# Streaming the whole v table as tiles for the first token group, instead of gathering its v rows

## The chip, the cores and the metric

The kernel runs on one core of one Trainium2 chip. The metric is the device time of one execution in microseconds (us), as the median of several runs. A profile is one execution recorded by the hardware profiler. The engines are PE (TensorE, matrix products), DVE (VectorE), ACT (ScalarE), POOL (GpSimd) and SP (SyncE), and 16 DMA engines move data between the device memory and the on-chip memory.

## The reference

Two transformer layers run one after the other on 512 tokens of width 1024. The change is in the last part only, a product-key expert layer (`peer_ffn`). Each token picks, in each of 8 heads, the 16 best of 16,384 experts; a row of table `u` gives each expert's gate, and a row of table `v` its output:

```python
idx = jnp.take_along_axis(cand_i..., best_pos, axis=-1)      # 8 heads x 16 experts a token
g = jax.nn.softmax(best_s, axis=-1)
pre = jnp.einsum('td,thkd->thk', xt, u[idx])
coef = g * jax.nn.gelu(pre, approximate=False)
out = x + jnp.einsum('thk,thkd->td', coef, v[idx])
```

Both tables are 16,384 x 1024 in float32, 64 MiB each. An expert's number is i * 128 + j, with i and j the two halves' keys.

## The kernel before

**Tiling.** Tokens lie on the 128 partitions, so there are four token tiles (t = 0 to 3), worked in two groups of two. A chunk k is one head of one token tile: k = 8t + head, 32 chunks in all. A chunk holds 16 expert slots. One gather brings, for one slot, the chosen row of `u` or `v` for each of 128 tokens: 128 rows of 4 KB, 512 KB. So 512 gathers read `u` and 512 read `v`.

**Who does what.** POOL issues all gathers in one queue, in the order of a written-out list `SEQ` (L433 ff.; the issuing line is L568). DVE multiplies a gathered `u` tile with the token's vector and sums it (`dots`, L1043), ranks scores and picks experts (`prep_top`, 986 to 1033), and for some `v` slots scales and adds the gathered rows itself (`added`, L1072). The other `v` slots go over PE (`weighted`; its matmuls stand at the helper line L1514): ACT writes a 128 x 128 diagonal matrix of the slot's coefficients (`diagonals`, L933), and PE multiplies it with the gathered 128 x 1024 tile in two matmuls of 512 columns, which add up in PSUM. In the profile one float32 matmul is two records. `on_vector` says which slots go to DVE: before, none of the first group (chunks 0 to 15), and 4 of 16 in chunks 16 to 28, 8 of 16 in the last three.

**Order.** The `u` gathers of chunks 0 to 15 run early, beside the dense layers and attention, through six buffers. Behind them the list has `v` chunks 0 to 2, then one `u` chunk and up to two `v` chunks in turn, until the last `v` chunks. These 768 later gathers go round a ring of 23 buffers: gather n takes the buffer of gather n - 23 and waits until that one is used up. Ten of the buffers lie in the attention's keys (`FIRST_KEYS`) and seven in the layer's scratch (`FIRST_LAYER`), and these wait for the end of the work that uses the place. POOL issues in order, so a gather that waits holds back all behind it.

**The end of the dense work.** PE ends its last dense matmuls (the expert scores of the last tile) at about 1326 us of the profile. From there on only the expert part is left; below it is called the tail.

## Time and profile before

| what | value |
|---|---|
| median of 3 runs | 2462.14 us (2461.33 to 2468.46) |
| the profiled execution's own time | 2447.57 us |
| its span in the trace | 2445.8 us |
| PE busy, share of the span | 1989.4 us, 81% |
| DVE busy | 1262.6 us, 52% |
| POOL busy | 1153.6 us, 47% |
| moved by the software (POOL) queue | 537.87 MB |
| mean rate over the span | 279 GB/s |

A stretch of the trace is read with the view by windows (busy time of each engine, number of records, granted PE clock as a share of full speed, DMA share, GB/s) and then with the timeline of one engine, where each row is a start, a duration, and in square brackets how long the engine had been idle and what ended it.

### The profile page before, as it was taken

The numbers are of one execution on the slowest core, as the hardware profiler recorded it, in microseconds if no ns is written. First come the engines' busy times: TensorE is split into PE (matmuls) and PEld (weight loads), VectorE is DVE, ScalarE is ACT, GpSimd is POOL, SyncE is SP. The second block draws the span as 40 slices with busy tenths as digits, with TensorE's granted clock in tenths as the row PEclk, the third lists the DMA queues.
The fourth block names the chain that finished last, engine by engine and source line by source line (L and its number), as shares of the span: only waits on it lengthen the run. The fifth ranks groups of instructions, "written<-read, shape, count | busy, mean of one in ns | idle before, by whom it ended". The sixth has DMA issues, their size and how long they took to land.

```text
span 2445.8 us, 20834 instructions
## 1 busy us (share of the span) xinstructions
PE 1989.4 (81%) x6988; PEld 1199.1 (49%) x6988; DVE 1262.6 (52%) x3046; ACT 501.1 (20%) x1238; POOL 1153.6 (47%) x1070
## 2 busy tenths in 40 slices
PE   6999999877699998877888988898888775574666
PEld 6777666566566673655567433343333232231222
DVE  0111125355878865799758533344433355445645
ACT  1111024312011111233312212222221121121211
POOL 2000000000335544657462577767677777767675
PEclk9999998888798898966999988998898898777878
DMA  5321343256576787988797999999999999999998
GB/s 154 103 104 69 120 143 137 78 207 215 206 275 230 265 308 290 382 286 280 270 365 266 331 356 362 359 334 354 363 354 357 372 332 332 399 349 403 354 378 309
DMA packets 209050, 681.88 MB, mean 279 GB/s; under 512 B 20145, under 2 KB 20145, under 8 KB 208945
## 3 DMA queue, kind: packets, MB, share of 16 engines
q0 software_dynamic: 148032, 537.87, 59.6%
q1 hardware_dynamic: 57968, 135.80, 15.4%
q10 hardware_dynamic: 2944, 6.89, 0.8%
q8 instruction: 57, 0.93, 0.1%
q14 instruction: 49, 0.39, 0.0%
HBM read 677.33 MB, written 3.15 MB: 278 GB/s over the span
## 4 chain that ended last, share of the span: by engine, by line
PE 62%; issue 12%; POOL 8%; DVE 7%; DMA 5%; another core or an unknown queue 3%; ACT 3%; ACTq 0%; SPq 0%; DVEq 0%; POOLq 0%; PEldq 0%
PE ps L1514 60%; POOL sb_arena L568 8%; DVE sb_arena L1043 3%; DMA sb_arena<-in_peer_u,sb_idx 1%; DMA sb_arena<-in_peer_v,sb_idx 1%; DMA sb_wring<-in_w_out 1%; DMA sb_gains<-in_norm_g 1%; DVE sb_arena L1454 1%; DMA sb_wring<-in_w_in 0%; ACT sb_arena L933 0%; DMA sb_wring<-in_w_up_attn 0%; PE ps L1823 0%; DVE sb_arena L1460 0%; DVE sb_stat L1439 0%
## 5 line engine op out<-in xcount | busy, mean ns | idle before, releaser
L1514 PE MATMUL ps<-sb_arena 128*128 128x512 f32 (+6 forms) x2736 | 1066.2, 542 | 312.8 <-issue 223.6
L568 POOL DMA_INDIRECT sb_arena<-in_peer_u,sb_idx x512 | 621.0, 1213 | 1036.5 <-DVE sb_idx L1033 499.6
L1514 PEld LDWEIGHTS ps<-sb_arena 128*128 128x128 f32 (+3 forms) x2736 | 504.7, 201 | 847.5 <-issue 776.0
L1043 DVE CUSTOM_DVE_ANT_0 sb_arena<-sb_arena 128x1024 f32<-128x1024 f32 x512 | 613.4, 1224 | 342.2 <-DMA sb_arena<-in_peer_u,sb_idx 295.7
L568 POOL DMA_INDIRECT sb_arena<-in_peer_v,sb_idx x512 | 520.3, 1016 | 239.8 <-issue 145.2
L1514 PE MATMUL ps<-sb_arena,sb_wring 128*128 128x256 f32 (+2 forms) x2816 | 536.8, 352 | 42.6 <-issue 32.7
L1514 PEld LDWEIGHTS ps<-sb_arena,sb_wring 128*128 128x128 f32 x2816 | 469.2, 201 | 97.9 <-issue 38.4
L933 ACT ACTIVATE sb_arena<-sb_ident,sb_coef 128x128 f32<-128x128 f32 x436 | 169.3, 399 | 889.4 <-PE ps L1514 397.2
L1514 PE MATMUL ps<-sb_wring,sb_arena 128*128 128x512 f32 (+3 forms) x608 | 258.1, 582 | 31.4 <-DMA sb_wring<-in_w_out 10.7
L1072 DVE SCALAR_TENSOR_TENSOR sb_arena<-sb_arena,sb_coef 128x1024 f32<-128x1024 f32 x76 | 97.7, 1286 | 215.9 <-DMA sb_arena<-in_peer_v,sb_idx 139.4
L1514 PEld LDWEIGHTS ps<-sb_wring,sb_arena 128*128 128x128 f32 (+1 forms) x608 | 117.7, 197 | 162.1 <-issue 119.7
L1252 DVE TENSOR_REDUCE sb_stat<-ps 128x1 f32<-128x144 f32 (+3 forms) x32 | 16.2, 506 | 91.2 <-PE ps L1514 91.0
L1823 PE MATMUL ps<-sb_ident,sb_arena 128*128 128x128 f32 x160 | 34.1, 364 | 19.0 <-DVE sb_arena L1468 18.7
L803 ACT COPY sb_arena<-ps 128x512 f32<-128x512 f32 x36 | 21.1, 585 | 138.6 <-PE ps L1514 117.0
L1043 DVE DVE_READ_ACCUMULATOR2_ANT sb_coef<- 128x1 f32 x512 | 42.0, 82 | 0.0
L1514 PE MATMUL ps<-sb_negc,sb_eye 8*128 8x16 f32 (+4 forms) x128 | 41.7, 403 | 0.0
L1823 PEld LDWEIGHTS ps<-sb_ident,sb_arena 128*128 128x128 f32 x160 | 24.8, 190 | 25.7 <-DVE sb_arena L1468 23.0
L1426 DVE SCALAR_TENSOR_TENSOR sb_arena<-ps,sb_stat,sb_arena 128x512 f32<-128x512 f32 x16 | 12.0, 750 | 46.3 <-PE ps L1514 38.3
L682 ACT ACTIVATE sb_arena<-ps,sb_stat 128x144 f32<-128x144 f32 (+3 forms) x32 | 17.2, 538 | 72.3 <-DVE sb_stat L1252 72.3
L690 ACT ACTIVATE sb_arena<-ps 128x512 f32<-128x512 f32 x16 | 9.6, 597 | 100.9 <-PE ps L1514 100.9
L827 ACT COPY sb_arena<-ps 128x128 f32<-128x128 f32 (+3 forms) x64 | 24.0, 427 | 29.5 <-PE ps L1823 28.8
L970 DVE SCALAR_TENSOR_TENSOR sb_newton<-sb_stat 128x1 f32<-128x1 f32 (+2 forms) x23 | 3.6, 157 | 49.5 <-ACT sb_stat L592 49.5
(220 smaller groups left out, 1071.8 us busy)
## 6 DMA issues: line engine op xcount, KB each, us to landing
sb_wring<-in_w_in SPq DMA_DIRECT2D x52, 1024.0 KB, 7.5
sb_wring<-in_peer_w_q SPq DMA_DIRECT2D x32, 1024.0 KB, 8.2
sb_wring<-in_w_o SPq DMA_DIRECT2D x16, 1024.0 KB, 6.9
sb_wring<-in_w_out SPq DMA_DIRECT2D x8, 1024.0 KB
sb_arena<-in_peer_u,sb_idx POOLq DMA_INDIRECT x512
sb_arena<-in_peer_v,sb_idx POOLq DMA_INDIRECT x512
sb_arena<-in_x ACTq DMA_DIRECT2D x8, 512.0 KB, 7.9
sb_wring<-in_w_up_pool SPq DMA_DIRECT2D x4, 1024.0 KB
```

Of the source, the lines that this page charges most:

```text
L568: nc.gpsimd.indirect_dma_start(gathered[buf(n)][:], None, table, bass.IndirectOffsetOnAxis(ap=idx[:, t, s:s + 1], axis=0))\
L682: nc.scalar.activation(Pb[:, n % 2, 0:w], s_ps[:, 0:w], ACT.Exp, bias=stat[:, 96 + n % 4:97 + n % 4], accum_out=stat[:, 100 + n % 4:101 + ...
L803: nc.scalar.copy(dst, src).then_inc(prep_evac, 1)
L827: nc.scalar.copy(PT2[:, kind, 0:i + 1, :], psum[:, 4 + kind, 0:(i + 1) * P].rearrange("p (a b) -> p a b", b=P))\
L933: nc.scalar.activation(diag[:, n % 4, :], ident[:], ACT.Copy, scale=coef[:, t, s:s + 1])\
L1043: nc.vector.tensor_tensor_reduce(out=gathered[buf(n)][:], in0=gathered[buf(n)][:], in1=xn[:, t % TG, :], scale=1.0, scalar=0.0, op0=ALU.mu ...
L1072: nc.vector.scalar_tensor_tensor(rows_of_tile(t), gathered[buf(n)][:], coef[:, t, s:s + 1], rows_of_tile(t), ALU.mult, ALU.add).then_inc(v ...
L1252: nc.vector.tensor_reduce(stat[:, 96 + n % 4:97 + n % 4], s_ps[:, 0:w], AX, ALU.max, negate=True)\
L1426: nc.vector.scalar_tensor_tensor(cols, psum[:, wo_bank(i, n), :], stat[:, 82 + kind:83 + kind], cols, ALU.mult, ALU.add).then_inc(x2_added, 1)
L1454: link(nc.vector.tensor_tensor_scan(suffix[:, w - 1::-1] if w == T else suffix[:, 0:w][:, ::-1], suffix[:, w - 1::-1] if w == T else suffi ...
L1514: return nc.tensor.matmul(o, l, r, start=start, stop=stop)
L1823: last = nc.tensor.transpose(psum[:, 4 + kind, j * P:(j + 1) * P], Pb2[:, kind, j * P:(j + 1) * P], ident[:])
```

## The change

For the first group (tiles 0 and 1) the `v` rows are no longer gathered. The whole `v` table is read once, as 128 tiles of 128 consecutive rows (512 KB each; tile i holds the experts with first key i). For each tile and each of the two token tiles PE multiplies a 128 x 128 weight matrix `dense_w` (row j: the coefficient of expert 128 i + j for each token) with the tile: 4 matmuls of 512 columns a tile (`dense`).

The weights are built on the chip, in two halves of 64 tiles. `split` and `ranks` bring the two keys and the coefficients of all slots onto the partitions by token. Then, 32 times for each half, for eight tokens: DVE makes eight 128 x 128 one-hot matrices of key j in one instruction and eight 128 x 64 one-hot matrices of key i scaled with the coefficient (`picks`), PE multiplies them (`build`, 8 matmuls of 64 columns), and ACT copies the result from PSUM (`spread`).

The list now has `u` 16 and 17, five times 12 tiles and a `u` chunk (18 to 22), 4 tiles, the second build (`b`) with `u` 23, `v` 16 and 17 worked between its steps, five times a `u` chunk, 12 tiles and a `v` chunk, and a remainder with the last 4 tiles. The tiles are issued by POOL in the same queue and go round the same ring as the gathers. The ring has 18 buffers until the last tile, and 33 behind it. `on_vector` now gives DVE 8 of 16 slots of every `v` chunk but 16 and 17.

```diff
+HALF = NK // 2
+PICK = 8
+BUILDS = TG * P // PICK
...
+        SEQ = [("u", 16), ("u", 17)]
...
+        for m in range(18, 23):
+            SEQ += stream(12) + [("u", m)]
+        SEQ += stream(4) + [("b", 0), ("u", 23), ("v", 16), ("v", 17)]
+        for m in range(24, 29):
+            SEQ += [("u", m)] + stream(12) + [("v", m - 6)]
+        SEQ += [("v", 23), ("u", 29)] + stream(4) + [("v", k) for k in range(24, 27)]
+        SEQ += [("u", 30), ("v", 27), ("v", 28), ("u", 31), ("v", 29), ("v", 30), ("v", 31)]
...
-            return k >= EARLY_CHUNKS and j % (2 if k >= CHUNKS - SHARED else 4) == 1
+            return k not in WITH_BUILD and j % 2 == 1
...
+        first_ring = list(KEYS) + list(RING)
+        second_ring = list(OVER) + list(SCORES) + first_ring
...
+            if n < OPEN:
+                return first_ring[(n - LATE) % len(first_ring)]
+            return second_ring[(n - OPEN) % len(second_ring)]
...
+            elif b in OVER:
+                eng.wait_ge(d_used, NK)
...
+                if kind == "d":
+                    gp.dma_start(gathered[buf(n)], table[k * P:(k + 1) * P, :]).then_inc(tile_landed[buf(n)], 16)
...
+            def spread(b):
...
+                act.wait_ge(pick_used, b + 1)
+                if half and q == 0:
+                    act.wait_ge(d_used, HALF)
+                nc.scalar.copy(dense_w[:, :, t, at_:at_ + PICK],
+                               psum[:, 4 + b % 2, :].rearrange("p (s i) -> p i s", s=PICK)).then_inc(spread_done, 1)
...
+            def picks(b):
...
+                    dve.wait_ge(pick_used, b - 1)
+                nc.vector.tensor_tensor(pick_j[b % 2], rank_t[:, TG + t, at_:at_ + PICK].unsqueeze(2)
+                                        .to_broadcast([P, PICK, NK]),
+                                        iota[:].unsqueeze(1).to_broadcast([P, PICK, NK]), ALU.is_equal)
+                for n in range(PICK):
+                    last = nc.vector.tensor_scalar(pick_a[:, b % 2, n, :], iota[:, HALF * half:HALF * (half + 1)],
+                                                   rank_t[:, t, at_ + n:at_ + n + 1],
+                                                   rank_t[:, 2 * TG + t, at_ + n:at_ + n + 1], ALU.is_equal, ALU.mult)
+                last.then_inc(pick_done, 1)
...
+            def build(b):
+                pe.wait_ge(pick_done, b + 1)
...
+                    pe.wait_ge(spread_done, b - 1)
+                for n in range(PICK):
+                    last = mm(psum[:, 4 + b % 2, n * HALF:(n + 1) * HALF], pick_j[b % 2][:, n, :],
+                              pick_a[:, b % 2, n, :], True, True)
...
+            def dense(i):
+                if i % HALF == 0:
+                    pe.wait_ge(spread_done, BUILDS * (i // HALF + 1))
...
+                for t in range(TG):
+                    for e in range(2):
+                        last = mm(sums_of(t)[:, e, :], dense_w[:, i % HALF, t, :],
+                                  gathered[buf(n)][:, 512 * e:512 * e + 512], i == 0, i == NK - 1)
+                last.then_inc(d_used, 1)
```

On PE the tail was one row of matmuls behind the last dense ones (`ps` is PSUM, `sb_arena` the large buffer that holds gathered tiles and diagonals). Before:

```order
L1514 MATMUL ps<-sb_arena 128x128 x4
L1514 MATMUL ps<-sb_arena,sb_wring 128x128 x32
L1514 MATMUL ps<-sb_arena 128x128 x8
L1514 MATMUL ps<-sb_arena 128x512 x872
L60 UNCONDITIONAL_BRANCH
```

After, the same place has the transposes of `ranks`, the 256 small matmuls of the first build, and then the first 60 tiles at four matmuls each, some of them in buffers that lie in the weight ring `sb_wring`:

```order
L1635 MATMUL ps<-sb_arena 128x128 x8
L2062 MATMUL ps<-sb_ident,sb_arena 128x128 x4
L2067 MATMUL ps<-sb_ident,sb_coef 128x128 x2
L1635 MATMUL ps<-sb_arena 128x64 x256
L1635 MATMUL ps<-sb_wring,sb_arena 128x512 x16
L1635 MATMUL ps<-sb_arena 128x512 x48
L1635 MATMUL ps<-sb_wring,sb_arena 128x512 x40
L1635 MATMUL ps<-sb_arena 128x512 x48
```

So the first matmul on `v` data now stands behind the whole first build. Further on, in the second build, each group of 8 small matmuls has one gathered slot of chunk 16 or 17 (2 matmuls) behind it.

On POOL, behind the 256 early gathers of `u`, three `v` chunks came before the next `u` chunk. Before:

```order
L568 DMA sb_arena<-in_peer_u,sb_idx 128x1024 x256
L568 DMA sb_arena<-in_peer_v,sb_idx 128x1024 x48
L568 DMA sb_arena<-in_peer_u,sb_idx 128x1024 x16
L568 DMA sb_arena<-in_peer_v,sb_idx 128x1024 x32
L568 DMA sb_arena<-in_peer_u,sb_idx 128x1024 x16
```

After, two `u` chunks follow at once (L626, a gather, has `sb_idx` as a source), and then 12 plain tile loads (L623) between `u` chunks:

```order
L626 DMA sb_arena<-in_peer_u,sb_idx 128x1024 x266
L626 DMA sb_wring<-in_peer_u,sb_idx 128x1024 x8
L626 DMA sb_arena<-in_peer_u,sb_idx 128x1024 x10
L626 DMA sb_wring<-in_peer_u,sb_idx 128x1024 x4
L623 DMA sb_wring<-in_peer_v 128x1024 x4
L623 DMA sb_arena<-in_peer_v 128x1024 x8
L626 DMA sb_arena<-in_peer_u,sb_idx 128x1024 x2
L626 DMA sb_wring<-in_peer_u,sb_idx 128x1024 x8
```

What moved is that no transfer of `v` data stands before the 289th of the queue, and that from there on transfers that PE frees and transfers that DVE frees alternate in blocks.

## Rows read from the trace of the kernel before

**Rows 1.** Windows: us, busy (records) PE PEld DVE ACT POOL, PEclk, DMA, GB/s:
```profile
1326.50:2445.80 1119.30, 840.38 (x1744) 350.27 (x1744) 522.97 (x1075) 218.03 (x517) 783.79 (x752) 0.86 0.95 355
1326.50:1800.00 473.50, 406.69 (x888) 174.21 (x888) 199.27 (x541) 102.50 (x248) 326.10 (x321) 0.92 0.95 355
...
2100.00:2400.00 300.00, 172.33 (x323) 68.06 (x321) 157.99 (x238) 47.67 (x108) 216.01 (x214) 0.76 0.97 377
```

**Rows 2.** The chain that ended last, 1640 to 1730 us: start, duration, what:
```profile
1650.41 4.86 issue
1655.27 3.78 PE ps L1514 x4
...
1665.06 56.29 PE ps L1514 x124
1721.35 4.89 issue
```

**Rows 3.** Timeline of POOL, buffers freed by PE, then a free one:
```profile
1408.10 0.94 POOL L568 DMA_INDIRECT sb_arena<-in_peer_v,sb_idx  x1 [0.78 <-PE ps L1514]
1409.82 0.94 POOL L568 DMA_INDIRECT sb_arena<-in_peer_v,sb_idx  x1 [0.78 <-PE ps L1514]
...
1420.26 0.93 POOL L568 DMA_INDIRECT sb_arena<-in_peer_v,sb_idx  x1 [0.31 <-issue]
```

**Rows 4.** Timelines of DVE and POOL: rankings' ends, first late u chunk:
```profile
1319.90 0.17 DVE L1033 CAST sb_idx<-sb_arena 128x16 uint32<-128x16 f32 x1
1328.74 0.17 DVE L1033 CAST sb_idx<-sb_arena 128x16 uint32<-128x16 f32 x1
...
1364.28 0.17 DVE L1033 CAST sb_idx<-sb_arena 128x16 uint32<-128x16 f32 x1
...
1374.27 0.93 POOL L568 DMA_INDIRECT sb_arena<-in_peer_u,sb_idx  x1 [1.28 <-PE ps L1514]
...
1379.27 1.23 DVE L1043 CUSTOM_DVE_ANT_0 sb_arena<-sb_arena 128x1024 f32<-128x1024 f32 x1 [14.82 <-DMA sb_arena<-in_peer_u,sb_idx]
```

**Rows 5.** Timelines of DVE and POOL, a stretch of dots back to back:
```profile
1971.84 1.22 DVE L1043 CUSTOM_DVE_ANT_0 sb_arena<-sb_arena 128x1024 f32<-128x1024 f32 x1
...
1972.98 1.22 DVE L1043 CUSTOM_DVE_ANT_0 sb_arena<-sb_arena 128x1024 f32<-128x1024 f32 x1
...
1971.88 1.98 POOL L568 DMA_INDIRECT sb_arena<-in_peer_v,sb_idx  x1 [0.31 <-issue]
```

**Rows 6.** Small DVE work: timeline near 1293 us, then groups by line:
```profile
1293.70 0.17 DVE L1015 TENSOR_SCALAR sb_arena<-sb_arena 128x16 uint32<-128x16 uint32 x1
1293.78 0.17 DVE L1016 TENSOR_SCALAR sb_arena<-sb_arena 128x16 uint32<-128x16 uint32 x1
...
1294.19 0.76 DVE L1020 TENSOR_TENSOR sb_arena<-sb_arena,sb_iota 128x256 f32<-128x256 f32 x2
...
L1085 DVE TENSOR_TENSOR sb_arena<-sb_arena,ps 128x1024 f32<-128x1024 f32 x4 | 4.9, 1217 | 3.3 <-PEq L1956 3.3
```

**Rows 7.** Small matmuls: timeline of PE, then groups of 0 to 60 us:
```profile
1316.88 7.31 PE L1514 MATMUL ps<-sb_arena,sb_wring 128*128 128x128 f32 x64
...
L1514 PE MATMUL ps<-sb_arena,sb_wring 128*128 128x16 f32 x59 | 8.5, 296 | 0.0
```

**Rows 8.** View by windows: full PE clock, and small matmuls of attention:
```profile
1600.00:1650.00 50.00, 50.00 (x118) 22.04 (x116) 24.87 (x65) 13.31 (x31) 35.60 (x35) 1.00 0.93 339
...
1050.00:1100.00 50.00, 35.51 (x141) 27.12 (x140) 44.54 (x95) 19.21 (x42) 29.41 (x21) 0.60 0.76 260
```

**Rows 9.** Single rows: a copy from PSUM, a plain DMA issued by POOL:
```profile
1326.13 0.58 ACT L803 COPY sb_wring<-ps 128x512 f32<-128x512 f32 x1 [0.42 <-PE ps L1514]
...
7.58 0.55 POOL L535 DMA_DIRECT2D sb_gain_row<-in_final_norm_g  x1
```

**Rows 10.** Timelines at the end: last gather, last sum:
```profile
2430.30 1.01 POOL L568 DMA_INDIRECT sb_arena<-in_peer_v,sb_idx  x1 [0.31 <-issue]
...
2441.45 1.22 DVE L1085 TENSOR_TENSOR sb_arena<-sb_arena,ps 128x1024 f32<-128x1024 f32 x1 [3.34 <-PEq L1956]
```

More of the change, by code:

```diff
@@ L942, in _ @@
                         gelu(CHUNKS - 1, CHUNKS)
[L943 to L944 removed]
+                    for _ in diagonals(m):
+                        pass
+                elif kind == "u":
                     for _ in range(2):
@@ L1115, in experts, with split @@
                             k_w += 1
-                        continue
-                    added(k)
-                    if k % H == 4 and k > H:
-                        finish(finished_tiles)
-                        finished_tiles += 1
-                for t in range(finished_tiles, NT):
-                    finish(t)
+                    elif kind == "b":
+                        rows_ = dots(23)
+                        for b in range(BUILDS):
+                            picks(BUILDS + b)
+                            if b < TOPK:
+                                next(rows_)
+                    elif kind == "v" and k not in WITH_BUILD:
+                        added(k)
+                        if k in (26, 27, 28):
+                            finish(k - 26)
+                finish(NT - 1)
+            def split():
+                dve.wait_ge(u_used, LATE)
+                both = idx[:, 0:TG, :].rearrange("p a b -> p (a b)")
+                nc.vector.tensor_scalar(rank_u[:, 0, :], both, 7, None, ALU.logical_shift_right)
+                link(nc.vector.tensor_scalar(rank_u[:, 1, :], both, NK - 1, None, ALU.bitwise_and))
+                nc.vector.tensor_copy(rank[:], rank_u[:]).then_inc(rank_ready, 1)
+            def picks(b):
+                half, q = divmod(b, BUILDS)
+                t, at_ = divmod(q * PICK, P)
+                if b < 2:
+                    dve.wait_ge(rank_copied, 2)
+                else:
+                    dve.wait_ge(pick_used, b - 1)
[7 more added lines that the diff above has]
+                last.then_inc(pick_done, 1)
             stream = experts()
@@ L1950, in weighted @@
                     for e in range(2):
-                        last = mm(psum[:, 4 + 2 * (t % 2) + e, :], diag[:, m % 4, :],
-                                  gathered[buf(n)][:, 512 * e:512 * e + 512], s == 0, s == last_row)
+                        last = mm(sums_of(t)[:, e, :], diag[:, m % 4, :],
+                                  gathered[buf(n)][:, 512 * e:512 * e + 512], row == 0, row == last_row)
                     last.then_inc(v_used, 1)
-                    if s == last_row:
+                    if row == last_row:
                         pe.wait_ge(v_used, m + 1)
                         pe.sem_inc(acc_done, 1)
-            for k in range(CHUNKS):
-                weighted(k)
+                    yield
+            ranks()
+            for b in range(BUILDS):
+                build(b)
+            for kind, k in SEQ:
+                if kind == "d":
+                    dense(k)
+                elif kind == "b":
+                    between = [weighted(k_) for k_ in WITH_BUILD]
+                    for b in range(BUILDS):
+                        build(BUILDS + b)
+                        next(between[0 if b < TOPK else 1])
+                elif kind == "v" and k not in WITH_BUILD:
+                    for _ in weighted(k):
+                        pass
 def kernel(**inputs):
```

217 lines of the change are left out of this document (144 added, 73 removed).

## The prediction

> **What bounds the kernel now.** I first read the view by windows over the tail [rows 1]. The reader is to see three things. The 752 gathers left after the dense work take 1119.3 us, 1.488 us each. In the late part it is 214 in 300 us, 1.40 us each, with the DMA share at 0.97 and PE busy only 172 us: there the DMA engines set the pace. In the first part it is 321 in 473.5 us, 1.475 us each, and PE is busy 407 us. PE's work in the tail is 872 matmuls (1744 records), busy 840 us. The chain of waits and the timeline of POOL say how the first part goes: 128 PE records, that is 32 slots, repeat every 71 us (1650.41 to 1721.35) [rows 2], and while PE works them POOL's issues stand 1.72 us apart, each released by PE, against 1.24 us where a buffer is free (0.93 and 0.31 ahead of it) [rows 3]. So one `v` slot costs PE 1.72 us (0.86 a matmul, full clock), more than a transfer costs the DMA engines, and the ring couples the two. The tail is bound by transfers, but only as long as the ring lets them run ahead.
>
> **What the change removes.** 256 gathers of `v` go, 128 tile loads of the same size come: 640 late transfers instead of 768, 128 x 1.40 = 179 us less. If nothing else counted, the tail would shrink by that. PE's work does not shrink with it: a tile is four matmuls, 3.44 us, twice a slot, so 128 tiles cost PE 440 us, exactly what the 256 slots cost. The group 2 slots on PE go from 180 to 144 (248 us), since DVE takes 112 instead of 76.
>
> **What it adds, step by step, on the time axis of the trace.** Up to 1326 us nothing of weight changes.
>
> 1. *First dots.* DVE ends its last ranking of this stretch at 1364.5 and then waited 14.8 us for the `u` chunk behind 48 `v` gathers [rows 4]. Now that chunk is first and has landed; with `split` (three short instructions, 2 us) dots start at 1366.5. Sixteen of them, whose starts lie 1.14 us apart [rows 5] (I take 1.15), end at 1385. In this time the DMA engines are idle once 18 buffers are full.
> 2. *First build.* A 1024-column comparison is not in the trace; the nearest rows are 1.217 us for a 1024-column addition and 0.38 for 256 columns, and small scalar operations start 0.08 us apart at 16 columns [rows 6]. I take 1.18 for the first and 0.11 for each of the eight 64-column ones: 2.1 us a step (bounds 1.8 and 2.9). 32 steps and the 16 dots among them: 67 + 18.4 = 85.6 us. PE's eight 64-column matmuls (16 records) lie between 16 x 0.114 = 1.8 us, from 128-column ones, and 16 x 0.144 = 2.3 us, from 16-column ones [rows 7]; I take 2.1. The copy is 0.58 us, nearest row [rows 9]. Both are hidden under DVE. With the last step's matmuls and copy the weights are ready at 1473. In 147 us only 50 transfers were asked for: 590 are left.
> 3. *Sixty tiles with `u` 18 to 22.* A block is 12 tiles and 16 gathers: DMA 28 x 1.40 = 39 us, DVE 16 x 1.15 and two rankings of 8.84 us [rows 4], 36 us, PE 12 x 3.44 = 41.3 us. PE is longest. The 28 places less the 18 buffers make the next block's first tile wait for the eleventh tile of this one (37.8 us); it lands 5.0 us after its issue (1374.27 to 1379.27 [rows 4]), so PE has a hole of 1.5 us, taken as 2.5. Five blocks are 219 us: 1692. POOL's tile issue is at 0.55 us no limit [rows 9]. Four more tiles, 14 us: 1706.
> 4. *Second build.* PE does both: 2.1 for the small matmuls and 1.72 for a slot of chunk 16 or 17, 32 times, 122 us; DVE needs 3.25 in the first half and 2.1 in the second and is hidden. With the last copy: 1830. The DMA engines need 67 us of it; about 398 transfers are left.
> 5. *Five times `u`, 12 tiles, `v`.* 44 transfers, 62 us. But during the 41.3 us in which PE works through 12 tiles only 12 places come free, one each 3.44 us. When it turns to the `v` slots, 15 transfers stand before the next tile: 1.7 + 14 x 1.40 and 5 to land, 26 us, of which PE's eight slots fill 13.8. So PE waits 12 us and the period is 26 + 41.3 = 67.3, and about 2.5 more since after a pause four records took 3.78 us instead of 1.72 [rows 2]: 70. From 1830: 5 + 41.3 to the first `v`, then 4 x 70, is 2156.
> 6. *The rest.* 30 transfers to the last tiles (44 us), landing, and four tiles of which the last ends 63 us on, at 2219. The first buffer behind `OPEN` waits for all tiles, so the DMA engines idle 15 us. Then 160 gathers at 1.40 and the reload of `x2r` (2.8 us) with 5 us to land: 2450. In the trace the end of the span is some 7 us behind the last landing (sum at 2441.45, span 2445.8 [rows 10]).
>
> The span comes to 2457 us against 2445.8, 11.4 us more. The profiled execution was 2447.57 us, 1.8 beyond its span, and 0.6% under the median of 2462.14; I put the 11.4 on the median: **2474 us**. What the 179 us pay for is the two builds (147 us with 50 transfers, 138 us with 52) and 8 us a period at step 5.
>
> How POOL fares while DVE is busy: with dots back to back a gather keeps POOL 1.98 us instead of 0.94 [rows 3, 5], 2.29 a gather with the 0.31 ahead of it. In the second build 48 issues at 2.29 are 110 us, below PE's 122, so my sum does not move. The Trainium skill, SBUF — State Buffer, "Who interferes with whom", says that a DVE instruction with two SBUF inputs, or a `tensor_scalar` in a two-port mode, shuts GpSimd out for its whole length. By that rule, the trace agrees for the two-input dots; it shows no stream of `tensor_scalar`. By that page a gather could wait for a whole step of `picks`.
>
> **Rivals.**
>
> *A. The ring hardly holds: transfers bound the tail.* For it: the late part runs at 1.40 us with a ring of 23 [rows 1]. Against it: POOL rows released by PE, and a ring of only 18. Steps 3 and 4 without their pauses end at 1817, 398 transfers at 1.40 add 557, and 12 for landing and end: 2386 in span, 2402 us. It decides if the next tile at step 5 lands within the 13.8 us of the `v` slots instead of 26. The Trainium skill, DMA: Bandwidth & Descriptors, "Issuing engines are not separate DMA queues", holds that the issuing engine makes no difference to the rate, and by it alone one queue would be no loss. This is the case on the other side, since it ends faster than before by 2.4%.
>
> *B. PE's clock falls in the builds.* In attention, with 128-column matmuls, the granted clock was 0.60 while PE was busy 35.5 of 50 us [rows 8]; with 512-column ones it was 1.00 at full load. At half clock a build is 4.2 us instead of 2.1: the first phase goes from 86 to 134 us, the second from 122 to 189 if the slots keep their pace. Added, 115: 2589 at worst, and if half of the time is at low clock, 2530. Against it: in the second build every other piece is 512 columns. It decides once a step is above DVE's 2.7 us.
>
> *C. POOL is shut out by the picks.* The 1.98 us row is an issue held through about one dot [rows 5]. If one is held through a whole step of 2.1 us and then takes 1.24, 48 issues are 160 us, 38 more than PE needs: 2512. Against it: the 64-column operations are short and may leave gaps.
>
> **How the numbers follow.** My forecast with its own range of 2440 to 2505 has 0.42; A 0.28, B 0.18, C 0.12. About 0.3% (7 us) is what a measurement of this kernel can tell from no change: under 2454.7 is faster, over 2469.5 slower. Of my own case I give 0.08 to faster, 0.12 to same, 0.22 to slower (the sum leaves out pauses of about 5 us that nothing in the profile explains, as the 4.86 us in [rows 2], so it errs low). Faster is then 0.28 + 0.08 = 0.36, same 0.12 with 0.01 of the rivals' edges, slower 0.51. The bounds of the unknown costs: a pick step at 1.8 takes 10 us off step 2, at 2.9 adds 26; transfers at 1.488 instead of 1.40 add 14 at step 6; no holes at steps 3, 5 and 6 take 60 off. Below, the range goes to the middle of A, 2395; above, into B, 2550. Outside are the faster half of A and the upper third of B, some 2 in 10.
>
> **What would show it.** Right: a first build from 1385 to 1473 with DVE nearly full and the DMA share below 0.4; tiles at 3.44 us each with the clock near 1.00 behind it; a second build of 122 us; five periods of 70 us with PE idle 10 to 12 us in each; DMA share 0.97 only behind the last tile; and 67 MB fewer moved in all. Wrong: small matmuls above 0.2 us a record (B); POOL rows above 2 us in the builds (C); periods of 62 us with full DMA share (A). A tile load that moves slower than a gather, or a pick step far above 2.1 us, would break the sum itself.

## The result and the profile after

| | before | after |
|---|---|---|
| median | 2465.24 us (2461.33 to 2468.46, 4 runs) | 2498.73 us (2492.45 to 2523.2, 4 runs) |
| profiled execution, its span | 2447.57, 2445.8 us | 2492.45, 2490.6 us |
| software queue moved | 537.87 MB | 470.75 MB |

The ratio is 1.0164 with a 95% interval of 1.0126 to 1.0202: slower, clear of no change, though the interval does not tell whether by more or less than 2%. I had put 2474 us (0.5%). The 67 MB that were to go have gone. In the two profiled executions the difference is 44.8 us of span against the 11.4 of the prediction. That overstates the loss: the profiled execution before lies 18 us under its median and the one after 6 us under its own, and the medians are 33.5 us apart.

The view by windows of the kernel after, cut at the borders of the change's stages (columns as in [rows 1]):

```profile
1326.00:1385.00 59.00, 24.83 (x181) 24.47 (x179) 57.26 (x185) 4.87 (x9) 31.18 (x25) 0.65 0.62 200
1385.00:1490.00 105.00, 103.05 (x470) 100.92 (x469) 103.49 (x303) 17.67 (x31) 13.71 (x15) 0.50 0.29 92
1490.00:1717.00 227.00, 223.06 (x512) 97.42 (x513) 188.72 (x545) 18.75 (x31) 116.51 (x136) 0.99 0.82 307
1717.00:1851.00 134.00, 116.92 (x641) 81.22 (x640) 111.30 (x311) 29.81 (x67) 75.60 (x57) 0.95 0.68 230
1851.00:2144.00 293.00, 227.62 (x512) 99.45 (x512) 133.73 (x191) 29.94 (x63) 174.97 (x188) 0.89 0.87 317
2144.00:2260.00 116.00, 88.66 (x193) 38.70 (x194) 40.93 (x52) 9.29 (x21) 56.50 (x58) 0.87 0.79 300
2260.00:2490.60 230.60, 133.09 (x256) 47.30 (x254) 126.79 (x140) 33.04 (x75) 172.46 (x155) 0.86 0.97 368
```

[rows 1] has the same view of before. There the DMA share of the tail was 0.95, so the DMA engines stood idle for 0.05 x 1119 = 56 us. After, the lengths times one less the share add up to 20.6 + 74.5 + 40.9 + 42.9 + 38.1 + 24.4 + 6.9 = 248 us. That is 192 us more idle time, against 147 us less busy time (1063 to 916): the sum is the 45 us. (The shares are rounded, so each total is good to some 6 us.) The first build alone is 75 of it, and there PE and DVE are both full, PE at clock 0.50.

The first build in the timelines of PE and DVE: four steps of PE as one row, and a pick step of DVE with the dot behind it.

```profile
1403.89 14.08 PE L1635 MATMUL ps<-sb_arena 128*128 128x64 f32 x64 [0.18 <-DVE sb_arena L1241]
1418.16 2.18 PE L1635 MATMUL ps<-sb_arena 128*128 128x64 f32 x9 [0.19 <-DVE sb_arena L1241]
...
1403.75 1.23 DVE L1237 TENSOR_TENSOR sb_arena<-sb_arena,sb_iota 128x1024 f32<-128x1024 f32 x1
1404.89 1.87 DVE L1241 TENSOR_SCALAR sb_arena<-sb_iota,sb_arena 128x64 f32<-128x64 f32 x8
1406.67 1.22 DVE L1126 CUSTOM_DVE_ANT_0 sb_arena<-sb_arena 128x1024 f32<-128x1024 f32 x1
1407.81 0.09 DVE L1126 DVE_READ_ACCUMULATOR2_ANT sb_coef<- 128x1 f32 x1
```

The reader is to see three things. On PE there are 14.27 us from start to start for 64 records, 3.57 us a step and 0.22 a record (predicted 2.1 and 0.13). PEld, which loads the 128 x 128 weights of each of these matmuls, is as full as PE (100.92 of 105 us above). And on DVE a pick step takes 1406.67 - 1403.75 = 2.92 us (predicted 2.1): the 128x1024 comparison starts the next instruction after 1.14 us, as forecast (1.18), but each 128x64 `tensor_scalar` takes 0.223 us and not 0.11. With a dot in every second step DVE needs 3.5, PE 3.57.

The start of the second build, on PE and POOL:

```profile
1717.13 1.89 PE L1635 MATMUL ps<-sb_arena 128*128 128x64 f32 x16
1732.72 3.62 PE L1635 MATMUL ps<-sb_wring,sb_poolw 128*128 128x512 f32 x4 [13.69 <-DMA sb_wring<-in_peer_v,sb_idx]
1736.17 1.90 PE L1635 MATMUL ps<-sb_arena 128*128 128x64 f32 x16
1737.90 1.94 PE L1635 MATMUL ps<-sb_wring,sb_poolw 128*128 128x512 f32 x4
...
1726.75 0.94 POOL L626 DMA_INDIRECT sb_wring<-in_peer_v,sb_idx  x1 [0.30 <-issue]
```

PE stands 13.69 us, because the first gather of `v` 16 is issued at 1726.75, behind the sixteen of `u` 23, which POOL issues one by one from 1704.70 on without waiting for a buffer. At full clock a build step is 1.73 us on PE (1736.17 to 1737.90) and a slot 1.77.

The late periods, from the timeline of PE: the first tile of the second to fifth block of twelve, and the last four tiles.

```profile
1924.33 15.41 PE L1635 MATMUL ps<-sb_wring,sb_arena 128*128 128x512 f32 x32 [17.91 <-DMA sb_wring<-in_peer_v]
1997.47 2.93 PE L1635 MATMUL ps<-sb_arena 128*128 128x512 f32 x3 [16.52 <-DMA sb_arena<-in_peer_v]
2068.34 12.07 PE L1635 MATMUL ps<-sb_wring,sb_arena 128*128 128x512 f32 x21 [13.28 <-DMA sb_wring<-in_peer_v]
2144.02 16.50 PE L1635 MATMUL ps<-sb_arena 128*128 128x512 f32 x32 [17.69 <-DMA sb_arena<-in_peer_v]
2236.34 4.63 PE L1635 MATMUL ps<-sb_arena 128*128 128x512 f32 x5 [20.88 <-DMA sb_arena<-in_peer_v]
```

The starts lie 73.1, 70.9 and 75.7 us apart (predicted 70) and PE waits 13 to 18 us (predicted 12), and 20.88 ahead of the last four.

What the first of these waits consists of, on PE (the last slots ahead of it) and on POOL:

```profile
1901.11 5.31 PE L1635 MATMUL ps<-sb_wring,sb_poolw 128*128 128x512 f32 x12
...
1905.99 1.17 POOL L626 DMA_INDIRECT sb_arena<-in_peer_u,sb_idx  x1 [0.30 <-issue]
...
1916.37 0.98 POOL L626 DMA_INDIRECT sb_wring<-in_peer_u,sb_idx  x1 [0.30 <-issue]
1917.35 2.21 POOL L623 DMA_DIRECT2D sb_wring<-in_peer_v  x4
```

By the ring of 18 the tile takes the buffer of PE's last slot (`v` 18, slot 14), which is done at 1906.42. At that moment seven `u` gathers stand ahead of the tile, the first of them just begun. None waits for a buffer (0.30 us ahead of each), but they follow one another at 1.0 to 2.1 us, and the tile is issued at 1917.35, 10.9 us late. It needs another 7.0 us to land. In all five late waits the tile is issued 6.7 to 13.9 us behind the end of that slot, 51.9 us together.

The steps of the prediction, in the profiled executions:

| step | predicted | measured | difference |
|---|---|---|---|
| 1 dots end | 1385 | 1372.3 | -12.7 |
| 2 first build | 88 us | 117.7 us | +29.7 |
| 3 sixty-four tiles | 233 us | 227 us | -6 |
| 4 second build | 124 us | 134 us | +10 |
| 5, 6 to the last tile | 389 us | 402 us | +13 |
| 6 rest | 238 us | 237.8 us | 0 |
| span | 2457 | 2490.6 | +33.6 |

Two of the steps came out shorter than predicted by 18.7 us and three longer by 52.7: part of the error cancelled.

### The profile page after: what moved, and what is told of

Same layout as the page of the kernel before. It is cut to its first block, busy times and chain, and to the rows that moved or that the text cites. A ratio compares the mean times of both kernels' runs of the same rounds, so it can differ in the third digit from the quotient of the medians.

```text
span 2490.6 us, 22672 instructions
## 1 busy us (share of the span) xinstructions
PE 2064.3 (83%) x7874; PEld 1335.0 (54%) x7874; DVE 1495.3 (60%) x3661; ACT 423.8 (17%) x1012; POOL 1009.9 (41%) x942
## 3 DMA queue, kind: packets, MB, share of 16 engines
q0 software_dynamic: 129600, 470.75, 52.3%
q1 hardware_dynamic: 57968, 135.80, 15.1%
q8 instruction: 63, 1.03, 0.2%
## 4 chain that ended last, share of the span: by engine, by line
PE 58%; DVE 15%; POOL 12%; DMA 7%; issue 7%; ACT 2%; ACTq 0%; another core or an unknown queue 0%; SPq 0%; DVEq 0%; POOLq 0%
PE ps L1635 57%; POOL sb_arena L626 9%; DVE sb_arena L1126 4%; POOL sb_wring L626 4%; DVE sb_arena L1241 2%; DMA sb_arena<-in_peer_v 1%; DVE sb_arena L1237 1%; DMA sb_arena<-in_peer_u,sb_idx 1%; DMA sb_wring<-in_w_out 1%; DMA sb_gains<-in_norm_g 1%; DMA sb_wring<-in_peer_v 1%; DVE sb_arena L1575 1%; DVE sb_wring L1126 1%; DMA sb_wring<-in_peer_v,sb_idx 0%; DMA sb_wring<-in_w_in 0%
## 5 line engine op out<-in xcount | busy, mean ns | idle before, releaser
L626 POOL DMA_INDIRECT sb_arena<-in_peer_u,sb_idx x405 | 523.8, 1293 | 1043.2 <-DVE sb_idx L1116 544.1
L1635 PE MATMUL ps<-sb_arena 128*128 128x64 f32 (+9 forms) x2576 | 651.8, 412 | 133.6 <-DMA sb_arena<-in_peer_v 58.3
L1635 PEld LDWEIGHTS ps<-sb_arena 128*128 128x128 f32 (+4 forms) x2576 | 435.8, 221 | 341.9 <-issue 185.2
L1126 DVE CUSTOM_DVE_ANT_0 sb_arena<-sb_arena 128x1024 f32<-128x1024 f32 x405 | 483.9, 1223 | 79.0 <-DMA sb_arena<-in_peer_u,sb_idx 72.8
L1635 PE MATMUL ps<-sb_wring,sb_arena 128*128 128x512 f32 (+3 forms) x1072 | 467.8, 595 | 64.3 <-DMA sb_wring<-in_peer_v 32.6
L626 POOL DMA_INDIRECT sb_arena<-in_peer_v,sb_idx x166 | 186.7, 1125 | 136.4 <-PE ps L1635 71.2
L1635 PE MATMUL ps<-sb_arena,sb_poolw 128*128 128x512 f32 (+1 forms) x388 | 185.5, 614 | 37.7 <-DMA sb_arena<-in_peer_v,sb_idx 32.7
L626 POOL DMA_INDIRECT sb_wring<-in_peer_u,sb_idx x107 | 121.5, 1136 | 121.4 <-PE ps L1635 74.7
L1635 PE MATMUL ps<-sb_wring,sb_poolw 128*128 128x512 f32 x204 | 101.1, 630 | 75.1 <-DMA sb_wring<-in_peer_v,sb_idx 47.2
L1126 DVE CUSTOM_DVE_ANT_0 sb_wring<-sb_wring,sb_arena 128x1024 f32<-128x1024 f32 x107 | 129.5, 1225 | 38.1 <-DMA sb_wring<-in_peer_u,sb_idx 33.8
L626 POOL DMA_INDIRECT sb_wring<-in_peer_v,sb_idx x90 | 97.3, 1081 | 78.4 <-PE ps L1635 40.1
L1241 DVE TENSOR_SCALAR sb_arena<-sb_iota,sb_arena 128x64 f32<-128x64 f32 x512 | 120.2, 328 | 0.0
```

What stands on the lines that cost most here:

```text
L626: nc.gpsimd.indirect_dma_start(gathered[buf(n)], None, table, bass.IndirectOffsetOnAxis(ap=idx[:, t, at_:at_ + 1], axis=0))\
L1126: nc.vector.tensor_tensor_reduce(out=gathered[buf(n)], in0=gathered[buf(n)], in1=xn[:, t % TG, :], scale=1.0, scalar=0.0, op0=ALU.mult, op ...
L1241: last = nc.vector.tensor_scalar(pick_a[:, b % 2, n, :], iota[:, HALF * half:HALF * (half + 1)], rank_t[:, t, at_ + n:at_ + n + 1], rank_t ...
L1635: return nc.tensor.matmul(o, l, r, start=start, stop=stop)
```

## The experiments

The experiments ran on three other chips, four kernels a chip, each with runs of the kernel before. On them the kernel before takes 2344.54, 2356.86 and 2348.39 us instead of 2465, so kernels are compared by their ratio to it on their own chip, or among those of one chip. The chips differ in the changed kernels too: behind the last tile the traces of the first of these chips (experiments 1 to 4) take 226 to 229 us, those of the changed kernel 238 and 239 us on two other chips. Absolute times of different chips are so to be compared only to some 10 us.

**1. A smaller ring.** The four last buffers of the first ring stay unused until the last tile.

```
-        first_ring = list(KEYS) + list(RING)
-        second_ring = list(OVER) + list(SCORES) + first_ring
+        first_ring = list(KEYS) + list(RING)[:4]
+        second_ring = list(OVER) + list(SCORES) + list(KEYS) + list(RING)
```

> Four of the 18 buffers of the first ring (up to the last tile) are left unused until that point; nothing else changes. If the ring sets the pace of the blocks of twelve tiles, each period of 73 us grows towards 73 x 18/14 = 94 us and the five of them with the five of 42 us cost 100 us or more: about 2600 us. If TensorE and the landing time of a tile set it, with buffers to spare, the time stays at 2495 to 2510 us. My own: between, the late periods grow by some 8 us each, about 2540 us.

2721.45 us, ratio 1.161 (1.1555 to 1.1667). The largest part of the loss is where none of the theories had it: the second build takes 254 us. PE, POOL and DVE in the second build:

```profile
1822.98 3.47 PE L1635 MATMUL ps<-sb_wring,sb_poolw 128*128 128x512 f32 x4 [8.76 <-DMA sb_wring<-in_peer_v,sb_idx]
1826.28 1.90 PE L1635 MATMUL ps<-sb_arena 128*128 128x64 f32 x16
1836.93 3.75 PE L1635 MATMUL ps<-sb_wring,sb_poolw 128*128 128x512 f32 x4 [8.76 <-DMA sb_wring<-in_peer_v,sb_idx]
...
1832.64 0.94 POOL L626 DMA_INDIRECT sb_wring<-in_peer_v,sb_idx  x1 [13.02 <-DVE sb_coef L1126]
...
1828.22 1.23 DVE L1237 TENSOR_TENSOR sb_arena<-sb_arena,sb_iota 128x1024 f32<-128x1024 f32 x1 [9.81 <-PE ps L1635]
```

It is a closed loop: DVE's dot frees the buffer, POOL issues the `v` gather at 1832.64, PE gets it at 1836.93, does slot and build (to 1844), and only that lets DVE pick again. A turn takes 14 to 17 us, the longer ones where PE's build runs at 3.5 us instead of 1.9. With 18 buffers the gather for slot b takes the buffer that dot b - 2 frees; with 14 it is dot b + 2, which stands behind pick b + 2, and that waits for build b, just ahead of slot b on PE. The stretch between the builds grows from 228 to 306 us, the late periods only from 73 to 78. So the ring matters, but 2540 us as I had it and the 2600 of the proportional theory were both far too low: the price is not in proportion to the size, it jumps where a gather comes to depend on the step that needs it.

**2. Another queue for the tiles.** SyncE issues the 128 tiles, in the same buffers and behind the same waits.

```
             for n in range(GATHERS):
+                if kind == "d":
+                    continue
                 wait_buffer(gp, n)
...
+            for k in range(NK):
+                n = place["d", k]
+                wait_buffer(sp, n)
+                sp.dma_start(gathered[buf(n)], a["peer_v_2"][0][k * P:(k + 1) * P, :])\
+                    .then_inc(tile_landed[buf(n)], 16)
```

> The 128 tiles are issued by SyncE in place of GpSimd, into the same buffers in the same order of the ring and behind the same waits; GpSimd passes over them. If the shared queue costs the time (a gather stands behind a tile that waits for its buffer, or a tile behind gathers), the waits of TensorE for a tile (6.6 to 7.1 us a period) go and the five late periods fall from 73 to about 66 us: about 2460 us. If the ring or TensorE sets the pace and not the queue, the time stays within 7 us of 2498.

2446.82 us, ratio 1.042 (1.0377 to 1.0458); the changed kernel has 1.057 (below), 36 us more by the ratios. (The 6.6 to 7.1 us in what I expected was the landing of a tile alone; the whole wait is the 13 to 18 us above.) From the list of waits from 1851 to 2253 us, of the changed kernel and then of this one (us in total, times, longest):

```profile
PE ps L1635 <- DMA sb_arena<-in_peer_v: 55.7, 4, 20.9
...
PE ps L1635 <- DMA sb_wring<-in_peer_v: 31.2, 2, 17.9
```

```profile
PE ps L1639 <- DMA sb_arena<-in_peer_v: 21.0, 4, 7.2
...
PE ps L1639 <- DMA sb_wring<-in_peer_v: 14.2, 2, 7.4
```

PE's waits for tiles fall from 86.9 to 35.2 us, by 51.7, which is what the tiles were issued late before (51.9). The stretch from the first tile behind the second build to the end of the last tile falls from 402 to 350 us. DMA share and rate over it, of after and of this kernel:

```profile
1851.00:2253.00 402.00, 315.47 (x704) 137.65 (x704) 174.66 (x242) 39.23 (x84) 226.03 (x239) 0.89 0.85 312
```

```profile
1865.00:2215.00 350.00, 315.86 (x704) 138.00 (x704) 171.50 (x237) 38.81 (x84) 189.35 (x176) 0.94 0.94 358
```

Ring and order are the same, so this part of the loss is the one queue: a tile whose buffer was free stood behind gathers that POOL had yet to issue. The edit also moves the tiles from the software queue to the hardware queue of the profile (software 470.75 to 403.64 MB, hardware 135.80 to 202.92), but a faster path is not what helps: PE's five waits are still 5.9 to 7.4 us, as long as the 6.6 to 7.1 us of landing alone before.

The edit has a price elsewhere that I had not expected. The stretch between the builds grows from 228 to 245 us, with 14.9 us of waits for tiles in it instead of 3.9. No run tells why. So 51 us won late, 6 in the second build and 17 lost early make the 36 to 40.

**3. No builds.** Picks, build matmuls and spreading copies go; what stands in for them is in the expectation.

```
-                            for b in range(BUILDS):
-                                picks(b)
-                                if b % 2:
-                                    next(rows_)
+                            nc.vector.memset(dense_w[:, HALF // 2:HALF], 0.0).then_inc(pick_done, 1)
+                            yield from rows_
...
-            for b in range(BUILDS):
-                build(b)
```

> Both builds of the dense weights are left out (the picks, the 128x64 matmuls and the spreading copies; the weights are whatever eight copies and one memset put there, so the output is not the reference's); the dots, the tiles and the diagonal slots stay. If the builds carry the loss, the first falls from 118 us to some 20 (sixteen dots at 1.14, or the memset) and the second from 134 us to the 16 x 2 slots at 1.76 = 56: 2498 - 98 - 78 = about 2325 us. If a full DMA takes over, less is won: the tail moves about 323 MB, 864 us at 374 GB/s, which would still allow 2210, so I expect 2320 to 2370. If the late dense part or the ring carries the loss, over 2430.

2337.01 us, ratio 0.9957 (0.9931 to 0.9983). Against the changed kernel's 1.0572 that is 0.0615 x 2350 = 145 us: the price of both builds, as they lie on the path (the weights of this kernel are not the real ones, so it stands for a time alone). It also says what the rest is worth: freed of its builds the kernel is only 0.4% faster than the kernel before on this chip. Its window over the late periods:

```profile
1700.00:2100.00 400.00, 314.24 (x700) 137.62 (x701) 164.73 (x224) 33.62 (x73) 218.84 (x237) 0.89 0.85 315
```

0.85 and 315 GB/s, as in the changed kernel (0.87 and 317): the periods do not come from the builds.

**4. Faster picks.** The eight `tensor_scalar` become two operations of 128x512.

```
-                for n in range(PICK):
-                    last = nc.vector.tensor_scalar(pick_a[:, b % 2, n, :], iota[:, HALF * half:HALF * (half + 1)],
...
+                each = [P, PICK, HALF]
+                link(nc.vector.tensor_tensor(pick_a[:, b % 2], rank_t[:, t, at_:at_ + PICK].unsqueeze(2)
+                                             .to_broadcast(each),
+                                             iota[:, HALF * half:HALF * (half + 1)].unsqueeze(1).to_broadcast(each),
+                                             ALU.is_equal))
+                nc.vector.tensor_tensor(pick_a[:, b % 2], pick_a[:, b % 2],
+                                        rank_t[:, 2 * TG + t, at_:at_ + PICK].unsqueeze(2).to_broadcast(each),
+                                        ALU.mult).then_inc(pick_done, 1)
```

> The eight 128x64 compare-and-multiply operations of a pick step (1.79 us) become one compare and one multiply of 128x512 (estimate 2 x 0.6 us). If TensorE at half clock sets the first build (3.56 us a step), only the 16 steps of the second build fall in which VectorE was last (4.07 to 3.53 us): 9 us less, 2490. If VectorE set the first build too, 48 steps lose 0.5 us each: 24 us less, 2474.

2477.22 us, ratio 1.0566 (1.0496 to 1.0636), not to be told from the changed kernel by the ratio. The absolute time is near the 2474 of the theory that VectorE sets the first build, but the changed kernel did not run on this chip, and the trace says otherwise. The first build went only from 113.9 to 109.5 us (first to last 128x64 matmul). The second went from 131.8 to 129.0, where I had expected 9 us: the step behind the 14 us hole now runs at half clock (3.52 us for sixteen records). The window of the first build:

```profile
1385.00:1485.00 100.00, 100.00 (x471) 100.00 (x471) 89.56 (x121) 17.56 (x30) 14.80 (x19) 0.50 0.33 104
```

PE and PEld have no gap at all and DVE has 10%: at clock 0.50, PE sets the first build.

**5, 6. Both kernels on one chip.** Unchanged copies.

> The kernel before, unchanged, for its profile on the chip on which its time is 2344 us and not 2465. If the gathers of the tail are what differs (the 752 of the tail take 1119 us in the first profile), the dense part ends at 1326 us here too and the tail is some 1015 us; if everything is faster by 5%, the dense part ends at about 1260 us.

> The changed kernel, unchanged, beside the kernel before on this chip. If its time follows the kernel before (the same 5%), 2375 us; if its tail is set by TensorE, VectorE and the ring, which are no faster here, 2480 to 2500 us. The second is what the run with the fast picks (2477 us on the chip of the first four experiments) points to.

The kernel before: 2357.03 us in one run (median of the seven others 2356.86). The kernel after: 2494.24 us, ratio 1.0572 (1.0521 to 1.0623). So the change costs 1.6% on one chip and 5.7% on another, and it is the kernel before that differs by 108 us. Its gathers from 1400 to 2300 us, as a window and as POOL's groups (mean ns of one, idle before and what ended it):

```profile
1400.00:2300.00 900.00, 692.70 (x1524) 297.75 (x1523) 454.01 (x917) 197.75 (x459) 689.23 (x679) 0.89 1.01 396
```

```profile
L568 POOL DMA_INDIRECT sb_arena<-in_peer_v,sb_idx x433 | 436.5, 1008 | 133.8 <-issue 121.4 <-PE ps L1514 12.4
```

396 GB/s against 355 in [rows 1], and POOL nearly never waits for a buffer here: it is as fast as it can issue. The dense part ends 10 us later than in the first profile (1336.0 against 1326.1). In the four traces of kernels with the order of before it ends at 1326 to 1337 us, in the ten with the new order at 1335 to 1343, so the change may cost some of this. It is not on the path of the sum, since DVE's rankings and dots last until 1372.

**7. A larger matmul in the first build.** The fast picks, and behind each build step one 128x512 matmul into a bank that nobody reads.

```
                 last.then_inc(pick_used, 1)
+                if b < BUILDS:
+                    mm(psum[:, 7, :], ident[:], gain_row[:, 0:512], True, True)
```

> The fast picks, and in the first build one 128x512 matmul more per step, into a bank that nobody reads. If the low clock of the first build (0.50 with TensorE busy 99% on 128x64 matmuls) comes from these small matmuls, the larger one lifts it: a step is 1.77 + 0.88 = 2.65 us on TensorE, VectorE's 2.4 + 0.57 = 3.0 us is last, and the first build falls from 114 to about 96 us; with the second build's 9 us about 2465 us. If the clock stays at 0.50, a step is 3.5 + 1.7 = 5.3 us, the build 168 us, and the time some 55 us longer than with the fast picks alone (2530).

2466.22 us, ratio 1.0463 (1.0434 to 1.0493), where 2465 was expected. The first build takes 97.9 us. Its window, and DVE's pick step:

```profile
1375.00:1465.00 90.00, 83.25 (x538) 64.06 (x538) 87.18 (x117) 17.56 (x30) 15.43 (x18) 0.99 0.37 120
```

```profile
1401.49 1.22 DVE L1237 TENSOR_TENSOR sb_arena<-sb_arena,sb_iota 128x1024 f32<-128x1024 f32 x1
1402.62 0.68 DVE L1241 TENSOR_TENSOR sb_arena<-sb_arena,sb_iota 128x512 f32<-128x512 f32 x1
1403.34 0.69 DVE L1245 TENSOR_TENSOR sb_arena<-sb_arena 128x512 f32<-128x512 f32 x1
1403.95 1.22 DVE L1126 CUSTOM_DVE_ANT_0 sb_arena<-sb_arena 128x1024 f32<-128x1024 f32 x1
```

PE is given more work and gets done sooner: the clock is 0.99 instead of 0.50, PE has 7% of slack, and DVE's 2.46 us and half a dot set the pace (3.06 a step). The low clock came with the small matmuls, not with idle time, since PE was 98 to 100% busy at 0.50.

**8. `u` 23 and `v` 16 in turns.** The changed kernel, with these two chunks' gathers issued u, v, u, v.

```
...
+                if (kind, k) == PAIR[1]:
+                    order_of_dmas += [(*item, j) for j in range(TOPK) for item in PAIR]
...
```

> The changed kernel with the gathers of u 23 and v 16 issued in turns, and nothing else. If the hole of 13.7 us ahead of the second build's first slot is the latency of the first v gather behind sixteen u gathers, it falls to a few us, and the second build, whose slots then no longer wait for a buffer that a dot has just freed, falls from 132 towards 32 x 3.53 = 113 us plus the picks' excess in its first half: together 15 to 25 us less than the changed kernel (ratio 1.050 where that has 1.057). If the ring gives it back later: no change.

2472.6 us, ratio 1.0501 (1.045 to 1.0552). PE at the start of the second build:

```profile
1718.13 1.89 PE L1642 MATMUL ps<-sb_arena 128*128 128x64 f32 x16
...
1719.86 1.94 PE L1642 MATMUL ps<-sb_wring,sb_poolw 128*128 128x512 f32 x4
```

The hole is gone and the second build takes 116.5 us instead of 131.8 (first to last 128x64 matmul), 15.3 us less. The ratio is the forecast one, but its interval overlaps that of the changed kernel on another chip (1.0521 to 1.0623). So the times make it likely, and do not show, that the ring gives nothing of it back.

**9. All four edits.** Fast picks, the larger matmul, tiles by SyncE, `u` 23 and `v` 16 in turns.

> Four edits together: fast picks, the larger matmul in the first build, the tiles issued by SyncE, and the gathers of u 23 and v 16 issued in turns (u, v, u, v) in place of u 23 first, so that the second build's first slot does not wait for its gather. From the changed kernel's 2490: 18 for the first build, 9 for the picks of the second, 45 for the tiles (measured), 14 for the hole ahead of the second build: about 2405 us if they add up. If the ring of 18 gives each gain back, over 2440. Either is slower than the kernel before on the chip where that takes 2344 us.

2414.62 us, ratio 1.0246 (1.0216 to 1.0276), beside 1.0572 of the changed kernel on the same chip: 80 us less, where 86 were expected (18 + 9 + 45 + 14). They add up: experiments 2, 7 and 8 lower the ratio by 0.0154, 0.0109 and 0.0071, together 0.0334, and all at once by 0.0326. It is still slower than the kernel before there; it was not run on a chip where that takes 2465 us.

**10. Half of the rows on VectorE, alone.** The kernel before with one line changed.

```
-            return k >= EARLY_CHUNKS and j % (2 if k >= CHUNKS - SHARED else 4) == 1
+            return k >= EARLY_CHUNKS and j % 2 == 1
```

> The kernel before with one part of the change: of every v chunk from the sixteenth on, 8 of 16 rows are added by VectorE (before: 4 of 16, in the last three chunks 8), and no tiles. In the kernel before on a chip where it takes 2357 us GpSimd never waits and spends 0.98 us and 0.30 between on a gather (409 GB/s); in the last stretch of the changed kernel it does not wait either and spends 1.11 + 0.30 (372 GB/s). If it is VectorE's larger share that lengthens GpSimd's gathers, this kernel is some 200 gathers x 0.13 = 30 us to, with all late gathers, 75 us longer than the kernel before: ratio 1.013 to 1.03. If not, 1.00, or under 1 where TensorE is relieved.

2366.89 us, ratio 1.0067 (1.0035 to 1.0098), where 1.013 to 1.03 was expected. POOL's gathers are longer (window and group as in 5, from the slowest of ten runs):

```profile
1400.00:2300.00 900.00, 600.54 (x1272) 246.55 (x1270) 507.76 (x946) 169.34 (x390) 698.84 (x656) 0.86 1.00 384
```

```profile
L568 POOL DMA_INDIRECT sb_arena<-in_peer_v,sb_idx x416 | 440.6, 1059 | 128.8 <-issue 118.5 <-PE ps L1514 10.2
```

1059 ns against 1008 for a gather of `v`, 384 GB/s against 396; in experiment 11, on this chip, with the share of before and a ring of 18, it is 993 ns. So this part of the change costs 16 us of its own where POOL sets the pace, half of the low end of what I expected.

**11. The kernel before with a ring of 18.**

```
-            return n % EARLY_BUFS if n < LATE else (n - LATE) % NB
+            return n % EARLY_BUFS if n < LATE else (n - LATE) % 18
```

> The kernel before with a late ring of 18 buffers in place of 23, which is what the changed kernel has until its last tile. If the ring of 18 by itself slows a stream of gathers, a tail of 1029 us grows by up to 23/18, over 100 us (ratio 1.05); if the ring hurts only where two engines in lock-step hold it (the builds), the ratio is within 1.00 and 1.01. I expect 1.01.

2376.15 us, ratio 1.0111 (1.0066 to 1.0156). A ring of 18 costs a plain stream of gathers 26 us. What 18 instead of 23 costs the changed kernel no run shows; experiment 1 has the step from 18 to 14 alone.

**12. Fewer rows on VectorE at the end.** Experiment 9, with 4 of 16 rows on VectorE in the chunks `v` 23 to `v` 28.

> The four edits of the run with everything together, and in the chunks v 23 to v 28 only 4 of 16 rows are VectorE's in place of 8. If VectorE's share lengthens GpSimd's gathers in the last stretch (1.41 us a gather against 1.28), 100 gathers x 0.1 = 10 us are won against that run (2414 us, ratio 1.025): ratio 1.020. If TensorE, with 12 slots of 1.76 us per 16 gathers (21 of 22 us) and a clock of 0.86, takes over, 10 us or more are lost: ratio 1.029 and over.

2401.45 us, ratio 1.0211 (1.0167 to 1.0256) against 1.0246 (1.0216 to 1.0276) on another chip. The intervals overlap, so a gain is likely but not shown by the times. The trace shows its mechanism. POOL's gathers of `v` from 2260 to 2390 us, of experiment 9 and of this one:

```profile
L637 POOL DMA_INDIRECT sb_arena<-in_peer_v,sb_idx x54 | 56.7, 1050 | 16.5 <-issue 16.2 <-PE ps L1649 0.3
```

```profile
L637 POOL DMA_INDIRECT sb_arena<-in_peer_v,sb_idx x56 | 56.9, 1015 | 17.1 <-issue 15.2 <-PE ps L1649 1.8
```

## Why the prediction was right in its sign and too small in its size

- The frame held: transfers won, two builds and the periods against it, the sum on the slow side. The 179 us won were 147 us of busy time of the DMA engines in the profiles. Experiment 3 confirms the frame from the other end: without the builds the ratio is 0.9957, so they are the difference between a little faster and slower.
- That the time lies near the forecast is in part luck. The errors of the steps partly cancel, and the result comes from the chip on which the kernel before takes 2465 us. On another chip the changed kernel takes nearly the same time and the kernel before 108 us less, so there the same change costs 5.7%, and no term of the sum had that.
- **Step 2 is the term that was mis-sized, by 29.7 us, on both of its sides.** The pick step was put at 2.1 us with an upper bound of 2.9, and it is 2.92: I took 0.11 us for a 64-column `tensor_scalar` from 16-column ones 0.08 apart [rows 6], and it is 0.223. The PE build was bounded by 1.8 and 2.3 from records that I took as of full clock, and it is 3.57 at clock 0.50. Either alone gives 32 x 2.92 + 16 x 1.14 = 112 or 32 x 3.57 = 114 us, so repairing one (experiment 4) brought 4 us and both (experiment 7) 16.
- **Rival B was true for the first build and false for the second.** I had given it as one case for both. What I held against it, that every other piece of the second build has 512 columns, fits experiment 7: with a 512-column matmul a step the clock is 0.99 in the first build too. Its sign, small matmuls above 0.2 us a record, came true (0.22), at 3.57 us a step instead of its 4.2. I should have split the rival at that sentence; B for the first build alone, 32 steps of 4.2 us in place of the 85.6, would have given 2523.
- Rival A failed by its own sign: the late periods are 71 to 76 us and not 62, at a DMA share of 0.87.
- Step 4 was 10 us too small. The sum had no term for the 13.69 us ahead of the first slot, although the order of the queue told it (sixteen `u` gathers stand ahead). In the first half of that build DVE at 2.92 + 1.14 = 4.06 us a step was longer than PE's 1.73 + 1.77, not hidden as I had it, for some 6 us in all. Against both, PE's 3.50 us a step instead of 3.82 gave 10 us back. Experiment 8 wins back the hole.
- Step 5 had the right mechanism, the block that frees one buffer per tile and the fifteen transfers that then stand ahead of the next tile, and a period of 70 us against 73. I priced those at 1.40 us each as if the DMA engines set the pace; they were POOL's issues, 1.63 us each from 1892.96 to 1917.35, with the DMA share at 0.80 to 0.89. Experiment 2 shows that 52 of the 87 us of waits are this shared queue, with ring and order as they were. The Trainium skill, DMA: Bandwidth & Descriptors, "Issuing engines are not separate DMA queues", says that DMAs of different issuing engines end on the same 16 DMA engines, and that issuing from several saves only the time to initiate them, usually small. The trace agrees that it is the issuing that was saved, but here it stood ahead of a waiting PE and was 7 to 14 us a time.
- Rival C had no place: but for that first slot, POOL's issues in the builds were not what PE waited for. Under the picks and dots a gather keeps POOL up to 1.96 us, as [rows 5] had it, and never a whole pick step of 2.92. The Trainium skill, SBUF — State Buffer, "Who interferes with whom", says that a DVE instruction with two SBUF inputs contends with a GpSimd instruction that reads SBUF. The trace of experiment 10 agrees: with more two-input additions on DVE POOL's gathers go from 1008 to 1059 ns, and there it costs time because POOL sets the pace.
- Step 1 was 12.7 us too late, because DVE's last ranking ahead of the dots ends at 1354.1 and not at 1364.5; no run tells why it is earlier. Sixteen dots from there take 18.3 us, against the 18.4 that I had. Step 6 was right to 1 us.
- What stays open: why the kernel before runs at 355 GB/s on one chip and at 396 on another. It is hardly the chip's DMA rate alone, since the last stretch of the changed kernel runs alike on both (375 GB/s from 2260 to 2390 us on the first, 369 on the other). No experiment told it apart, but the traces show where the time is.

From the list of POOL's waits from 1400 to 2300 us, of the first trace of the kernel before and of experiment 5 ("remote" is another core or a queue that the profile does not know):

```profile
POOL sb_arena L568 <- issue: 173.9, 535, 4.9
POOL sb_arena L568 <- remote: 49.9, 19, 5.5
```

```profile
POOL sb_arena L568 <- issue: 185.7, 609, 0.3
```

With the usual 0.30 us ahead of each gather taken off, the first trace has 55 us of pauses, up to 5.5 us long, whose cause it does not name; the other has none. With the somewhat longer gathers (1.05 us against 1.015) they account for most of the 66 gathers by which the first one is behind. What makes the pauses stays open.

## What to carry to other kernels

A saving of transfers is worth only what the new serial work leaves of it: write down for each new stage how long the DMA engines will have nothing to do, for that was the loss here (248 us of idle against 56). Where two engines hand small steps to each other through two buffers, price both at their worst and look for a second limit behind the first, since repairing one of two equal limits brings next to nothing (4 us here). Count the places between a waiting instruction and its transfer in an in-order queue: each costs its issue time even if nothing in it waits. Another queue for such transfers can win that back, but look at every stage, since here it won 51 us in one and lost 17 in another.

## What the runs showed of the hardware

- PE busy 98 to 100% with 128x64 fp32 matmuls was granted the clock 0.50 (1.2 GHz), and 0.99 (2.4 GHz) when one 128x512 matmul was added to every sixteen records. A 64-column record took 0.22 us at the one and 0.11 at the other (1.73 us for sixteen). The 128-column ones of [rows 7] take 0.11 us too, at full clock: half of the columns saved next to nothing, and in the first build the engine's weight loads were as full as its matmuls (100.92 and 103.05 of 105 us).
- A gather of 128 rows keeps POOL 0.94 us, with 0.30 between two, and up to 1.98 us under dots of DVE back to back [rows 5].
- A `tensor_scalar` with two per-partition scalars over 64 columns costs 0.223 us each in a row, a two-input operation over 512 columns 0.61 to 0.72 from start to start. Eight of the first (1.78) are dearer than two of the second (1.33), which do the same work.
- The kernel before differs by 5% between chips (2465 and 2344 us), and the changed one does not on the two chips where it ran (2499 and 2494). A ratio measured on one chip did not hold on the next.
